# A streaming encoder layer on one core: all early tokens of the output projection beside the recurrence, eight late half pieces behind it, and attention's dense pieces by tile

## What is computed

```python
h   = rmsnorm(x, norm_mix_pre)
c   = h @ w_in                       # RWKV-7 inputs | q | k | v | two branch gates
y_a = rwkv7(...)                     # recurrence over chunks of 64 tokens, 8 heads of 64
o   = diff_attention(q, k, v)        # 4 heads, softmax of two score maps, p1 - lam * p2
o   = rmsnorm(o, subln) * (1 - lam_init)
g_a, g_b = split(sigmoid(g_in + b_gate), 2)
mix = g_a * (y_a @ w_out_a) + g_b * (o @ w_out_b)
x   = x + rmsnorm(mix @ w_o, norm_mix_post)
u_g, u_v = split(rmsnorm(x, norm_ffn_pre) @ w_ffn_in, 2)
x   = x + rmsnorm((silu(u_g) * u_v) @ w_ffn_out, norm_ffn_post)
```

## Time and profile before

| | |
|---|---|
| median of 3 runs | 1032.37 us (1031.08 to 1033.18) |
| the profiled execution's own time | 1031.23 us |
| its span, first to last instruction | 1029.4 us |
| mean granted clock of TensorE | 0.996 |
| PE busy | 988.3 us (96%), 8886 matmul records |
| DVE, ACT, POOL busy | 447.5, 285.9, 556.1 us |
| attention's first four tiles | about 201 to 275 us |
| recurrence and fills | about 275 to 536 us |
| late pieces, w_o, norms | 536 to 626 us |
| FFN and down projection | 626 to 1029 us |

### The profile page before, as it was taken

One profiled execution on the slowest core, in us unless ns is written; L12 is line 12 of the kernel. 1 busy time (PEld: TensorE's weight loads), 2 busy tenths in 40 slices (PEclk: granted clock), 3 DMA queues, 4 the chain that ended last, 5 costly groups with the idle time before them and its releaser, 6 DMA issues.

```text
span 1029.4 us, 22159 instructions
## 1 busy us (share of the span) xinstructions
PE 988.3 (96%) x8886; PEld 936.0 (91%) x8886; DVE 447.5 (43%) x878; ACT 285.9 (28%) x810; POOL 556.1 (54%) x608
## 2 busy tenths in 40 slices
PE   5999999999999999999998999999999999999997
PEld 5999999988878887888897999999999999999996
DVE  5366478277644545656445254333333333200003
ACT  5213444255554133232211453010010001020101
POOL 6667899633455224143347632555555555565671
PEclk9999999999999999999999999999999999999999
DMA  8332332432223110160026411322332232232332
GB/s 247 87 88 77 83 82 63 129 113 74 67 75 89 34 33 33 33 207 22 27 68 196 136 53 52 100 82 81 90 94 81 82 100 83 75 95 75 96 92 88
DMA packets 138111, 89.63 MB, mean 87 GB/s; under 512 B 5386, under 2 KB 130032, under 8 KB 138032
## 3 DMA queue, kind: packets, MB, share of 16 engines
q1 hardware_dynamic: 129508, 73.11, 24.4%
q10 hardware_dynamic: 8524, 15.42, 4.3%
HBM read 79.32 MB, written 9.19 MB: 86 GB/s over the span
## 4 chain that ended last, share of the span: by engine, by line
PE 83%; DVE 7%; ACT 3%; issue 2%; POOL 2%; DMA 1%; SPq 1%; ACTq 0%; DVEq 0%; POOLq 0%
PE dense L1027 67%; PE side L1105 3%; DMA w_raw<-in_w_in 1%; PE side L929 1%; POOL w_lo L746 1%; DVE amax L1736 1%; PE side L979 1%; PE side L950 1%; PE side L1225 1%; PE side L1009 1%; PE side L940 1%; PE side L889 1%; PE side L1174 1%; POOL w_hi L741 1%; PE side L875 1%
## 5 line engine op out<-in xcount | busy, mean ns | idle before, releaser
L741 POOL TENSOR_SCALAR w_hi<-w_raw 128x256 fp32r<-128x256 f32 (+1 forms) x255 | 158.1, 639 | 350.0 <-PE dense L1027 335.0
L746 POOL TENSOR_TENSOR w_lo<-w_raw,w_hi 128x256 fp32r<-128x256 f32 (+1 forms) x255 | 318.8, 1272 | 9.8
L1027 PE MATMUL dense<-h_hi,w_hi 128*128 128x272 f32 (+2 forms) x1376 | 298.0, 295 | 3.2 <-POOL w_lo L746 1.6
L1027 PE MATMUL dense<-h_hi,w_lo 128*128 128x272 f32 (+2 forms) x1376 | 289.3, 289 | 0.0
L1027 PE MATMUL dense<-h_lo,w_hi 128*128 128x272 f32 (+2 forms) x1376 | 288.5, 288 | 0.0
L1027 PEld LDWEIGHTS dense<-h_hi,w_hi 128*128 128x128 f32 x1376 | 218.0, 189 | 13.6 <-issue 7.7
L1027 PEld LDWEIGHTS dense<-h_lo,w_hi 128*128 128x128 f32 x1376 | 218.5, 189 | 0.0
L1027 PEld LDWEIGHTS dense<-h_hi,w_lo 128*128 128x128 f32 x1376 | 217.2, 189 | 0.0
L1027 PE MATMUL dense<-S,w_hi 128*128 128x272 f32 (+2 forms) x648 | 109.3, 289 | 0.0
L1027 PEld LDWEIGHTS dense<-S,w_hi 128*128 128x128 f32 x648 | 92.1, 188 | 0.1
L1027 PE MATMUL dense<-S,w_lo 128*128 128x272 f32 (+2 forms) x324 | 68.2, 288 | 0.0
(11 more groups left out here) (275 smaller groups left out, 1393.2 us busy)
## 6 DMA issues: line engine op xcount, KB each, us to landing
w_raw<-in_w_ffn_in SPq DMA_DIRECT2D x44, 512.0 KB, 3.7
w_raw<-in_w_in SPq DMA_DIRECT2D x43, 512.0 KB, 3.7
w_raw<-in_w_ffn_out SPq DMA_DIRECT2D x16, 448.0 KB, 3.6
gates<-gst ACTq DMA_DIRECT2D x16, 272.0 KB, 2.1
w_raw<-in_w_ffn_out SPq DMA_DIRECT2D x8, 512.0 KB, 3.7
w_raw<-in_w_o SPq DMA_DIRECT2D x6, 512.0 KB, 4.1
w_raw<-in_w_out_a SPq DMA_DIRECT2D x5, 512.0 KB, 3.3
mb<-gates ACTq DMA_DIRECT2D x1, 2176.0 KB, 10.4
```

What stands on the lines that cost most here:

```text
L741: ins = nc.gpsimd.tensor_scalar(hi[:, q], raw[:, q], 1.0, 0.0, ALU.mult, ALU.add)
L746: ins = nc.gpsimd.tensor_tensor(lo[:, q], raw[:, q], hi[:, q].bitcast(F32), ALU.subtract)
L1027: ins = pe.matmul(acc[:, bk, 0:tn], w, r[:, t0:t0 + tn], start=first and n == 0, stop=final and n == 2)
```

## The change

Two things. In attention, the second quarter piece is no longer in every second head but in every head of tiles 2 and 3 and in none of tiles 0 and 1. In the output projection, `OUT_EARLY` is now all eight blocks; `outE` 6 and 7 come behind the last step of the recurrence, ahead of the late pieces. The late pieces are eight `outL` in the order 4 to 7, 0 to 3; the kind `outA` is gone, and with it the two-bank case of the mix (`mix_halves` becomes `mix_parts`). There is one weight unit more (129 for 128), and two `mixE` more.

```diff
--- before
+++ after
@@ -102,10 +102,10 @@
-OUT_EARLY = range(6)
-OUT_LATE = [("outL", i) for i in (2, 3, 4, 5, 0, 1)] + [("outA", 6), ("outA", 7)]
-LATE_BANK = {d: (n // 2 + 1) % 2 for n, d in enumerate(OUT_LATE) if d[0] == "outL"}
-MIX_PIECE = {d: sum(1 + (e[0] == "outA") for e in OUT_LATE[:n]) for n, d in enumerate(OUT_LATE)}
+OUT_EARLY = range(8)
+OUT_LATE = [("outL", i) for i in (4, 5, 6, 7, 0, 1, 2, 3)]
+LATE_BANK = {d: (n // 2 + 1) % 2 for n, d in enumerate(OUT_LATE)}
+MIX_ORDER = [d for d in OUT_LATE if d[0] == "outL"]
@@ -119,7 +119,7 @@
     if (_kind, _i) in OUT_LATE[0:4]:
         SEGS.append((next(u for u, w in enumerate(UNITS) if w[:2] == ("outE", _i // 2)), _kind, _i))
-    elif _kind in ("outA", "outB", "outE", "outL"):
+    elif _kind in ("outB", "outE", "outL"):
@@ -246,7 +246,7 @@
-    turns = [1] + [n for i in range(BH * SAMPLE) for n in (0, 1, i % 2)] + [2, 1, 1, 1, 1, 0, 1, 1, 1, 1, 1, 1]
+    turns = [1] + [n for i in range(BH * SAMPLE) for n in (0, 1, i // (2 * BH))] + [2, 1, 1, 1, 1, 0, 1, 1, 1, 1, 1, 1]
@@ -589,14 +589,11 @@
-    def mix_halves(d):
+    def mix_parts(d):
         i, acc = d[1], dps[BLOCK[d] % 2]
-        if d[0] == "outA":
-            cuts = [(bk * HALF, HALF, acc[:, bk, 0:HALF]) for bk in range(2)]
-        else:
-            cuts = [(2 * P, TOK - 2 * P, acc[:, LATE_BANK[d], 0:TOK - 2 * P])]
-        return [(S[:, i, 0, a:a + n], S[:, i, 1, a:a + n], ga[:, i, a:a + n], mb[:, i, a:a + n], c) for a, n, c in cuts]
+        a, n = WO_PART["A" if d[0] == "outL" else "B"][0:2]
+        return S[:, i, 0, a:a + n], S[:, i, 1, a:a + n], ga[:, i, a:a + n], mb[:, i, a:a + n], acc[:, LATE_BANK[d], 0:n]
@@ -1675,10 +1672,10 @@
         def mix_low(d):
-            for half, (hi, lo, _, _, acc) in enumerate(mix_halves(d)):
-                dve.wait_ge(s_["mix_hi"], MIX_PIECE[d] + half + 1)
-                ins = vec.scalar_tensor_tensor(out=lo, in0=acc, scalar=0.5, in1=hi.bitcast(F32), op0=ALU.mult, op1=ALU.subtract)
-            ins.then_inc(block_sem(d), 1)
+            hi, lo, _, _, acc = mix_parts(d)
+            dve.wait_ge(s_["mix_hi"], OUT_LATE.index(d) + 1)
+            vec.scalar_tensor_tensor(out=lo, in0=acc, scalar=0.5, in1=hi.bitcast(F32), op0=ALU.mult,
+                                     op1=ALU.subtract).then_inc(block_sem(d), 1)
@@ -2054,19 +2051,18 @@
-                elif kind in ("outA", "outL"):
+                elif kind == "outL":
                     dve.wait_ge(s_["ga_loaded"], 16)
                     block_full(dve, d)
-                    halves = mix_halves(d)
+                    _, _, gate, other, a2 = mix_parts(d)
                     block_landed(dve, ("outB", i))
-                    for _, _, gate, other, a2 in halves:
-                        V(vec.scalar_tensor_tensor(out=a2, in0=gate, scalar=1.0, in1=a2, op0=ALU.add, op1=ALU.mult))
-                        V.mark(vec.tensor_tensor(a2, a2, other, ALU.add), s_["mixed"], "mixed")
+                    V(vec.scalar_tensor_tensor(out=a2, in0=gate, scalar=1.0, in1=a2, op0=ALU.add, op1=ALU.mult))
+                    V.mark(vec.tensor_tensor(a2, a2, other, ALU.add), s_["mixed"], "mixed")
                     turn = OUT_LATE.index(d)
-                    if turn and OUT_LATE[turn - 1][0] == "outL":
+                    if turn:
                         mix_low(OUT_LATE[turn - 1])
-                    if kind == "outA":
+                    if turn == len(OUT_LATE) - 1:
                         mix_low(d)
```

More of the change, by code:

```diff
@@ L716, in _ @@
                 sp.dma_start(dst.rearrange("p (k n) -> p k n", k=KT), w_in[:, :, c0:c0 + P]).then_inc(raw_loaded[slot], 16)
-            elif kind in ("outA", "outB", "outE", "outL"):
+            elif kind in ("outB", "outE", "outL"):
                 w = w_ob if kind == "outB" else w_oa
@@ L1042, in dense @@
             if b >= 2 and part == 0:
-                pe.wait_ge(dense_read[b % 2], b // 2 - (kind == "outL"))
+                pe.wait_ge(dense_read[b % 2], b // 2 - (kind in ("outL",)))
             acc = dps[b % 2]
@@ L1050, in dense @@
                 pe.wait_ge(w_split, u + 1)
-                if kind in ("outA", "outB", "outE", "outL"):
+                if kind in ("outB", "outE", "outL"):
                     hi, lo = (o_hi, o_lo) if kind == "outB" else (y_hi, y_lo)
@@ L1054, in dense @@
                 elif kind in ("woA", "woB"):
-                    ops = [(k * P, S[:, k, 0, :], S[:, k, 1, :]) for _, k in OUT_LATE]
+                    ops = [(k * P, S[:, k, 0, :], S[:, k, 1, :]) for _, k in MIX_ORDER]
                 elif down:
@@ L1069, in dense @@
                     if d == ("woA", 0):
-                        block_landed(pe, OUT_LATE[n])
+                        block_landed(pe, MIX_ORDER[n])
                     if d == ("woB", 0) and n == 0:
@@ L1090, in dense @@
                     elif kind in ("outE", "outL"):
-                        places = [(LATE_BANK.get(d, 0), *WO_PART["B" if kind == "outE" else "A"][0:2])]
+                        places = [(LATE_BANK.get(d, 0), *WO_PART["A" if kind == "outL" else "B"][0:2])]
                     elif parts_ == BY_TOKENS:
@@ L1579, in _ @@
                     continue
-                if kind in ("outA", "outL"):
+                if kind == "outL":
                     turn = OUT_LATE.index(d)
-                    for half, (hi, _, _, _, acc) in enumerate(mix_halves(d)):
-                        act.wait_ge(s_["mixed"], MIX_PIECE[d] + half + 1)
-                        f_act(hi, acc, ACT.Copy, scale=0.5).then_inc(s_["mix_hi"], 1)
+                    hi, _, _, _, acc = mix_parts(d)
+                    act.wait_ge(s_["mixed"], turn + 1)
+                    f_act(hi, acc, ACT.Copy, scale=0.5).then_inc(s_["mix_hi"], 1)
                     if turn == 1:
```

## The result

| | before | after |
|---|---|---|
| median of 16 runs each | 1032.24 us | 1037.09 us |
| lowest and highest | 1030.27, 1033.21 | 1035.44, 1043.59 |
| ratio, 95% interval | | 1.0058 (1.0048 to 1.0067) |
| span of the profiled execution | 1029.4 us | 1035.7 us |

The account below looks back on a forecast made before the run. TensorE, 83% of the chain that ended last, was taken as the bound. Terms +2.7 - 4.7 + 2.2 + 0.2 = +0.4 us took the profiled 1031.23 to 1031.6 us, median 1032.8 us, range 1030.1 to 1035.3 us.

Parts of the forecast that it names:

- Attention: Attention's first four tiles: late heads cost +3.9 us, early heads give back 1.2; +2.7 us in all (-0.5 to +6.7).
- the wait of 0.86 us at 230.81: Attention: VectorE's chain waits there for TensorE; this was to come back, within about 1.2 us from the early heads.
- the hit priced at 0.5 us: Tiles 0 and 1: one VectorE scaling fewer slowed by GpSimd's subtraction, worth about 0.5 us, inside the attention bounds.
- Late pieces: Between recurrence and w_o: waits and low clock of 7.3 us go, 2.6 us replace them; -4.7 us (-3.5 to -5.2).
- the 0.4 us inside that block: First w_o block: 0.4 us lost in it before, counted among the 7.3 us that were to go.
- The wait ahead of that block: Before w_o's first block: TensorE waits for VectorE to write the low half of bank 0's block, about 1.6 us.
- The early pieces as cover: Ahead of the late pieces: two added early pieces hide GpSimd's later normalisation; price 0, 0.4 us to spare, 2.1 uncovered.
- woB 0's wait for the eighth mix: First w_o block for early tokens: it waits for the last early mix to be split; +2.2 us (1.9 to 2.8).
- The splits of w_o: GpSimd's splits of w_o's weights: at 3.5 us a unit, ready as TensorE wants them; +0.2 us (0 to 1.3).
- the term's upper bound: GpSimd's splits of w_o: up to 1.3 us if loads for the third to fifth unit, issued together, are slow.
- The clock: Rival: the 2.2 us wait ahead of w_o's early blocks brings clock 0.50; price 1.4 us, time 1034.2 us, chance 0.12.
- the sum of 0.4 us: Whole kernel: attention +2.7, late pieces -4.7, mix wait +2.2, splits +0.2 make +0.4 us on the profiled execution.

Follow-up runs that it names:

- the kernel with both mends and the gain's load moved: Changed kernel with attention as before, early mixes split in pairs, two residual loads one block later, gain load behind w_o's fourth block: 1028.33 us, ratio to before 0.9969.

## Why the prediction was wrong

**Attention: right in mechanism, 0.6 us short.** Foreseen +3.9 in the late heads and -1.2 in the early ones, +2.7 in all. Measured from the scores' row of head 8 (238.31 before, 236.88 after) to the recurrence: 41.46 us for 36.74, so +4.7, and -1.4 ahead of it; together +3.3. TensorE-bound late heads and waits of VectorE for scores were foreseen and are there. The early heads gave back what was foreseen but not where: the wait of 0.86 us at 230.81 stayed (0.88 at 230.17), and another of 0.88 us came at 213.71, so VectorE's chain was not unbroken. VectorE's scaling at the end of tile 0 takes 0.29 us instead of 0.82; that is the hit priced at 0.5 us.

**Late pieces: right.** No wait of 2.53 us any more and no low clock inside the pieces. Foreseen -4.3 us up to w_o's first block (the 0.4 us inside that block came on top), measured -4.1. The wait ahead of that block was 1.95 us, not 1.6.

**The early pieces as cover: right.** GpSimd's second group of the normalisation began at 538.97 and ended at 540.5, and the first late piece had no wait for y_lo.

**woB 0's wait for the eighth mix: right.** Foreseen +2.2 us, measured +2.2 in the wait, and its removal gave 3.3 us by the ratios with the clock behind it.

**The splits of w_o: the step that failed.** "By adding 3.5 us a unit they stand ready just as TensorE, at 3.54 us a block, wants them: +0.2 us (0 to 1.3...)". I took GpSimd's own time for its pace and left it no slack for a load. That time was short as well: 3.67 us for four units, 0.5 us in all. Before, its splits had a lead of 11.9 us on the first block (547.00 to 558.86), and waits of up to 5.2 us for `z` in them cost nothing. After, the lead is 5.3 us (552.76 to 558.02). Then two loads came late, 2.28 and 1.93 us, and TensorE lost 1.9 us at block 8 (+0.2 had stood in the sum). Worse for the sum, the gain of the late pieces was spent here: with GpSimd's chain as the bound, removing a wait ahead of w_o brought nothing, twice over. What I listed as the term's upper bound, the loads of three units issued together, was the right suspicion; the collision of the last unit's load with the residual's I had not looked for.

**The clock: the rival with too small a chance, and with too few places.** I gave 0.12 to a fall behind the wait ahead of w_o's early blocks. It came there (+1.5) and behind the wait ahead of w_o's first block too, which no rival had. That stretch is 1.2 us longer: 1.5 of low clock, less 0.3 of the 0.4 that the sum had rightly taken off. Those 0.4 us were no low clock: in the first block before, at a granted clock of 1.00, a weight load waited for the last low half (the row of PEld, the weight loads):

```profile
561.97 1.12 PEld L1027 LDWEIGHTS dense<-S 128*128 128x128 f32 x8 [0.36 <-DVE S L1680]
```

The first fall was hidden by GpSimd (without it TensorE would have waited longer at block 8), the second was not.

So the sum of 0.4 us would have been 0.4 + 0.6 (attention) + 0.2 (late pieces) + 1.7 (splits) + 1.6 (block 1: +1.2 where -0.4 stood) + 1.5 (clock at block 9) = 6.0, against 6.3 in the spans. The terms for the splits and for block 1 are read from starts and are not independent: GpSimd alone would have brought block 8 to 586.01 us. The medians moved by 4.9 us, less than the spans, because the profiled execution before lies 1.0 us under its median and the one after 0.4 us above.

What stays open: why a load of 512 KB takes 3.7 us in one place and 4.0 to 4.5 in another, why unit 3's load, with the same loads around it, takes 5.8, 5.7, 4.7 and 4.1 us in four kernels, and what decides whether the clock falls behind a wait.

## What to carry to other kernels

When a stage is shortened, ask of every engine that feeds it what lead it had and what is left of it: here GpSimd's lead fell from 11.9 to 5.3 us, and late loads that had cost nothing became the bound. A load that nobody waits for is not free when it shares the DMA engines with one that somebody does; moving one such load by 18 us (551.5 to 569.4) was worth more (1.8 us at the split in the trace, 1.6 us by the ratios) than removing a visible wait of 2 us on the busiest engine, which gave nothing. And before a wait is removed, look at what the next block waits for: the output part's gain of 1.5 to 3.7 us appeared only when the early mixes and the loads had been moved as well.

## What was not expected of the hardware

Over the fourteen profiles, TensorE had 19 waits of 1.95 to 2.63 us between 536 and 640 us. Behind 12 of them the granted clock fell to 0.50, behind 7 it did not, in the same kernel and at the same place too: the wait of 1.96 us ahead of w_o's first block was followed by it in four of seven profiles. Of 20 waits of 1.6 to 1.7 us 3 were. A fall costs about 1.5 us: the first block and the second up to its transposition took 7.98 us with it (558.02 to 566.00) and 6.49 us without (555.71 to 562.20 in the kernel with both mends and the gain's load moved). A wait of 2 us is thus worth some 3 us on average (2 and 12 of 19 times 1.5). The spread of the times goes with the clock. Of 25 runs of the kernel before on one chip, the nine with a mean granted clock of 0.997 or more took 1029.8 to 1031.1 us, the twelve with 0.995 or less 1031.4 to 1032.9. After the change the times spread over 8.2 us in 16 runs, before over 2.9; the two longest have the two lowest clocks (0.990 and 0.991), but two more falls make only some 3 us of that, and the rest is not explained.
